# Two unrolled layers, a prologue fed by token blocks, and 512-column up and down matmuls in the last layer

## What is computed

```python
h = concatenate([meta, x], axis=1)                      # 528 tokens
for l in range(2):
    xn = rms_norm(h, attn_norm_g[l])
    q, k, v, u = split(xn @ w_in[l])
    q, k = rope(rms_norm(q)) * q_scale, rope(rms_norm(k))
    h = h + concatenate([sliding_sink_attention(q, k, v, sinks[l]), multiscale_pool(u)]) @ w_out[l]
    xn = rms_norm(h, ffn_norm_g[l])
    g = causal_dwconv(xn @ w_gate[l], conv_w[l], conv_b[l])    # width 3, over tokens
    h = h + (gelu(g) * (xn @ w_up[l])) @ w_down[l]
return h[:, 16:]                                        # the meta tokens are dropped
```

## Time and profile before

| | us |
|---|---|
| three runs | 1168.80, 1163.15, 1167.52 |
| median | 1167.52 |
| span of the profiled execution (its own time was not taken apart from it) | 1165.8 |
| TensorE busy in it | 1125.1 (97%) |
| VectorE, ScalarE, GpSimd busy | 540.5, 472.4, 172.8 |

### The profile page before, as it was taken

The page is one execution under the profiler, slowest core; times in us unless marked ns, Lnnn a source line. Parts: engine busy times, 40 slices in busy tenths (PEclk is TensorE's granted clock), DMA queues, the critical chain, the costliest instruction groups (busy, mean ns, idle before and its releaser), DMA issues.

```text
span 1165.8 us, 21588 instructions
## 1 busy us (share of the span) xinstructions
PE 1125.1 (97%) x8850; PEld 1082.5 (93%) x8850; DVE 540.5 (46%) x663; ACT 472.4 (41%) x652; POOL 172.8 (15%) x138
## 2 busy tenths in 40 slices
PE   4899899999999999999969999999999999999997
PEld 3897699999999999999969876999999999999997
DVE  4666646445454545212157565455544554432222
ACT  3675524544444443111238643353434343421110
POOL 2362003000100010000043510121100110000000
PEclk9989989999999999999989897999999999999999
DMA  5211032322232232233221112223232323233211
GB/s 197 89 46 37 1 109 73 109 73 92 88 108 72 80 100 90 73 100 97 75 74 47 37 37 69 76 74 109 73 107 72 108 72 108 72 100 93 70 63 72
DMA packets 92828, 94.47 MB, mean 81 GB/s; under 512 B 3712, under 2 KB 91096, under 8 KB 92776
## 3 DMA queue, kind: packets, MB, share of 16 engines
q1 hardware_dynamic: 91728, 93.01, 25.0%
q10 hardware_dynamic: 1048, 0.76, 0.2%
HBM read 91.65 MB, written 2.10 MB: 80 GB/s over the span
## 4 chain that ended last, share of the span: by engine, by line
PE 92%; DVE 4%; ACT 2%; issue 2%; DMA 1%; SPq 0%; DVEq 0%; ACTq 0%
PE slot L429 83%; PE slot L573 2%; PE slot L576 2%; DVE x_lo L1009 2%; PE slot L544 1%; PE slot L555 1%; PE slot L481 1%; PE slot L464 1%; DMA x_in<-in_x 1%; DVE ms_work L1075 1%; PE slot L558 1%; DVE sink_all L999 0%; PE slot L667 0%; DVE v_T L1047 0%; ACT rot_s L815 0%
## 5 line engine op out<-in xcount | busy, mean ns | idle before, releaser
L429 PE MATMUL slot<-x_hi,w_hi 128*128 128x264 f32 x1728 | 368.7, 290 | 18.0 <-DVE x_lo L1009 17.9
L429 PE MATMUL slot<-x_lo,w_hi 128*128 128x264 f32 x1728 | 364.0, 288 | 0.0
L429 PE MATMUL slot<-x_hi,w_lo 128*128 128x264 f32 x1728 | 363.9, 288 | 0.0
L343 DVE TENSOR_TENSOR w_lo<-raw,w_hi 128x2048 fp32r<-128x2048 f32 (+2 forms) x86 | 192.8, 2242 | 252.6 <-ACT w_hi L334 252.6
L429 PEld LDWEIGHTS slot<-x_hi,w_hi 128*128 128x128 f32 x1728 | 276.5, 191 | 23.1 <-DVE x_lo L1009 20.7
L334 ACT ACTIVATE w_hi<-raw 128x2048 fp32r<-128x2048 f32 (+3 forms) x90 | 162.6, 1806 | 304.6 <-PE slot L429 297.0
L429 PEld LDWEIGHTS slot<-x_lo,w_hi 128*128 128x128 f32 x1728 | 275.3, 191 | 0.0
L429 PEld LDWEIGHTS slot<-x_hi,w_lo 128*128 128x128 f32 x1728 | 275.0, 191 | 0.0
L429 PE MATMUL slot<-m_hi,w_hi 128*128 128x264 f32 x704 | 143.0, 284 | 0.0
L429 PE MATMUL slot<-m_lo,w_hi 128*128 128x264 f32 x704 | 142.9, 284 | 0.0
L429 PE MATMUL slot<-m_hi,w_lo 128*128 128x264 f32 x704 | 142.6, 284 | 0.0
(11 more groups left out here) (137 smaller groups left out, 1085.8 us busy)
## 6 DMA issues: line engine op xcount, KB each, us to landing
raw<-in_w_gate SPq DMA_DIRECT2D x44, 512.0 KB, 4.4
raw<-in_w_up SPq DMA_DIRECT2D x44, 512.0 KB, 4.6
raw<-in_w_down SPq DMA_DIRECT2D x32, 512.0 KB, 4.0
raw<-in_w_in SPq DMA_DIRECT2D x20, 512.0 KB, 4.8
raw<-in_w_out SPq DMA_DIRECT2D x16, 512.0 KB, 4.0
raw<-in_w_down SPq DMA_DIRECT2D x16, 384.0 KB, 3.5
x_in<-in_x SPq DMA_DIRECT2D x4, 512.0 KB, 5.7
out<-y_out SPq DMA_DIRECT2D x8, 256.0 KB, 2.9
```

Source lines behind the costliest of these rows:

```text
L343: ins = nc.vector.tensor_tensor(w_lo[s][:, a:b], raw[s][:, a:b], w_hi[s][:, a:b].bitcast(f32), ALU.subtract)
L429: ins = nc.tensor.matmul(out_half, w[ws][:, r, cols], a[:, k, half * HALF:(half + 1) * HALF], start=first and n == 0 and w is w_hi and a i ...
```

## The change

Five things are done together.

1. The loop over the layers is written out on all engines (`for l in range(DEPTH)`); waits on counts have constants, and copies of the layer's parameters (`par`, `nsink`, `gain_next`, `gains_all`) go. The MLP and down loops stay.
2. In the last layer, up and down are made for the 512 real tokens: `dense(..., real=True)` writes 512 columns of one bank with one matmul. What works on up, conv, gelu, m and the down sums there takes 512 columns too (`t0 = N_META`). Gate keeps 528.
3. At the end of layer 0, after each pair of down tiles, ScalarE and VectorE make x_hi, x_lo, squares and sums of these two tiles for layer 1, and go on to the next layer's weight units 0 and 1 (`split_hi` and `split_lo` take a unit number past `UNITS`).
4. The sums of squares of both norms are made by VectorE (`add_square`), and GpSimd's low part of the first unit too.
5. The prologue goes by token blocks: eight transposes of block t fill slot t, ScalarE copies half to h and VectorE the other. The k half of the first weight unit is loaded before the third block and split ahead of the v half. q and k norm gains, the sinks and the large table are loaded from GpSimd's queue.

```diff
-    PROLOGUE = [2, 3, 2, 2, 1]
+    PROLOGUE = [1, 1, 1, 2, 1]
...
         def split_hi(act, l, unit, i=0, half=None):
+            if unit >= UNITS:
+                l, unit = l + 1, unit - UNITS
...
         @block.sync
+            kv_cols = blocks(w_in[0])[:, :, ATTN_WIDTH:ATTN_WIDTH + UC]
             for t in range(SEQ // P):
+                if t == 2:
+                    sp.dma_start(raw[0][:, :, 0:P], kv_cols[:, :, 0:P]).then_inc(kraw_loaded, 16)
                 sp.dma_start(x_in[:, t], x[0, t * P:(t + 1) * P, :]).then_inc(x_loaded[t], 16)
+            for a in (0, 4):
+                sp.dma_start(raw[0][:, a:a + 4, P:UC], kv_cols[:, a:a + 4, P:UC]).then_inc(raw_loaded[0], 16)
...
-            sp.wait_ge(par_loaded, 16 * 11)
-            with sp.Fori(0, DEPTH) as l:
+            for l in range(DEPTH):
...
+                if real:
+                    dst = [(slice(N_META, L), slot[s][:, 0, 0:SEQ])]
+                elif part is None:
...
             for k in range(KT):
-                s, feat = (2 + k) % 4, slice(k * P, (k + 1) * P)
...
+            for t in (0, 1, None, 2, 3):
+                if t is None:
+                    pe.wait_ge(par_loaded, 16 * 7)
+                    pe.wait_ge(qk_loaded, 16 * 4)
...
+                pe.wait_ge(x_loaded[t], 16)
+                if t == 3:
+                    pe.wait_ge(evac[3], 1)
+                for k in range(KT):
+                    ins = nc.tensor.transpose(slot[t][:, k // 4, (k % 4) * P:(k % 4 + 1) * P],
+                                              x_in[:, t, k * P:(k + 1) * P], ident)
+                ins.then_inc(filled[t], 1)
+            pe.wait_ge(h_copied, SEQ // P)
...
-            with pe.Fori(0, DEPTH) as l:
+            for l in range(DEPTH):
...
+                        dense(s, unit % 2, (n % 2) * P, eight, x_hi, x_lo, ready=ready if n == 0 else None,
+                              real=n >= 2 and l + 1 == DEPTH).then_inc(filled[s], 1)
...
-                                            m_hi, m_lo, first=n == 0, last=n == 2)
+                                            m_hi, m_lo, first=n == 0, last=n == 2, real=l + 1 == DEPTH)
...
         @block.gpsimd
-            def sum_squares(norm):
...
+            for src, r in ((q_norm_g, R_QG), (k_norm_g, R_KG)):
+                for half in range(2):
+                    pool.dma_start(par_in[r:r + 1, :, half * HEAD_DIM:(half + 1) * HEAD_DIM],
+                                   src.rearrange("(a l) d -> a l d", a=1)).then_inc(qk_loaded, 16)
...
+            pool.dma_start(cst[:, C_CNT:], const[:, C_CNT:]).then_inc(const_loaded, 16)
...
         @block.scalar
+            for t in range(SEQ // P):
+                if t == 2:
+                    act.wait_ge(kraw_loaded, 16)
+                    nc.scalar.activation(w_hi[0][:, :, 0:P], raw[0][:, :, 0:P], ACT.Copy).then_inc(khi_split, 1)
+                act.wait_ge(filled[t], ps.PROLOGUE[t])
...
+            for k in range(KT):
+                gain_hi(0, R_AG, k)
+            act.wait_ge(raw_loaded[0], 32)
+            nc.scalar.activation(w_hi[0][:, :, P:UC], raw[0][:, :, P:UC], ACT.Copy).then_inc(hi_split[0], 1)
+            split_hi(act, 0, 1)
+            for k in range(KT):
+                square(0, 0, k)
+            act.wait_ge(eps_ready, 1)
+            act.wait_ge(prep_ready, 1)
+            act.wait_ge(const_loaded, 16)
...
-                for unit in range(U_DOWN + 2, UNITS):
-                    split_hi(act, l, unit)
+                for j in range(4):
+                    for n in range(3):
+                        if n == 2 and l + 1 < DEPTH:
+                            for k in (2 * j, 2 * j + 1):
+                                act.wait_ge(evac[ps.slot(f"down{k}")], ps.before(f"down{k}", l) + 1)
+                                gain_hi(l + 1, R_AG, k)
+                                square(l + 1, 0, k)
+                        if U_DOWN + 3 * j + n + 2 < UNITS or l + 1 < DEPTH:
+                            split_hi(act, l, U_DOWN + 3 * j + n + 2)
...
         @block.vector
+            def add_square(l, norm, k):
...
+                        if n == 2 and l + 1 < DEPTH:
+                            for k in (2 * j, 2 * j + 1):
+                                gain_lo(l + 1, R_AG, k)
+                                add_square(l + 1, 0, k)
```

245 lines of the change are left out of this document (122 added, 123 removed).

## The result

| | before | after |
|---|---|---|
| runs, taken side by side on one chip | 4 | 4 |
| median, us | 1167.35 | 1126.32 |
| lowest to highest, us | 1163.15 to 1168.80 | 1124.39 to 1129.72 |
| ratio to the kernel before, 95% interval | | 0.9652 (0.9621 to 0.9682) |
| profiled execution: its time, its span | (not apart), 1165.8 | 1127.35, 1125.4 |

The account below looks back on a forecast made before the run. TensorE's own matmul stream was taken to bound the kernel; savings of 30.0 + 12.0 + 11.3 = 53.3 us cut the span from 1165.8 to 1112.5, and 1.7 more gave 1114.2 us, range 1107 to 1130.

Parts of the forecast that it names:

- 512 columns: Last layer's up and down: at 1056 places one 215.8 ns matmul replaces two costing 244.2 ns, saving 30.0 us.
- the column mean: Plain float32 row, 528 column times per weight load, 222.5 ns for 220.0 of columns; gave the 2.5 ns added to 213.3.
- My mechanism: In TensorE's stream, a weight load lasts as long as 264 columns and they interfere; a longer matmul should hide its load.
- Rival 1: In the 512-column matmuls, the 12.1 ns are fixed per matmul, 1124.3 us (15%), or a price per column, 1136.4 us (6%).
- The seam: Between the two layers, 23.75 us for 96 matmuls that need 11.7: no wait left, clock never falls, 12.0 us saved.
- the cover that was counted: At the seam, matmuls of the first six rows, 4.4 us, cover VectorE's 3.3 us for the last two tiles.
- The prologue: Up to the first normalisation: the root begins at 34.6 in place of 45.92, saving 11.3 us.
- Rival 3: The prologue's loads come late; if the root begins at 42 rather than 34.6, the time is 1122 us; 10%.
- Rival 2: Tiles don't come as single matmuls, or the seam stays because x_lo is late on VectorE: 12 less, 1126; 3%.
- rival 4: Second layer's code, fetched anew, stalls TensorE: over 12 stalls lose everything, twenty give 1202 us; 2%.
- The attention: Stretches from each layer's first root or k and v to its gate: forecast saving 0.

Follow-up runs that it names:

- the control: The changed kernel once more, letter for letter, measured beside its successors on one chip: 1130.91 us, ratio 0.9673 to the kernel before.
- the fastest version: Changed kernel with last-layer gate for tokens 12 to 527, sums ahead of unit 1, parameters' wait behind the root, k's weights behind the third block: 1124.17 us.

## Why the prediction was right, and where it was wrong

**512 columns, 30.0 forecast, 13.6 measured: the step that failed.** The count (1056 places) and the price of what was removed (244.2 ns) were right, the price of what was added was not: 231.3 ns in place of 215.8. I took the column mean as the nearest row "in columns per load". It is plain float32, and its column times go at 0.42 ns; a float32r column takes 0.44. The nearest row has to be nearest in number format first. The trace of before offered one float32r length at the high clock, 264, from which fixed and per-column share cannot be told apart; the bounds were 225.4 and 236.8, and that their middle, 231.1, is near the measured price is luck. My mechanism, that at 264 columns the weight load and the columns get in each other's way and that a longer matmul hides its load, fails with it: about 116 of the 122.1 ns are columns, and what comes on top of 0.417 ns a column grows from 12.1 ns at 264 columns to 18.0 at 512 (231.3 - 213.3), where a load that is hidden would have made it shrink. A floor by the load was seen at 128 columns (111.8 ns) and not at 256 (117.6). Rival 1 (15% and 6%) was the right rival, with its two forms mixed. The time lay in the range because the range reached past this rival; the point rested on the wrong price.

**The seam, 12.0 forecast, 12.3 measured.** The x_lo of the last two tiles ran from 575.65 to 577.7 beside the cover that was counted, the clock stayed at 1.00, and the first k matmul followed the last down matmul in the stream. The forecast of the whole was sound because it was made from a measured piece against its steady-state price. The prediction named its causes (idle time, half clock, x_lo slowed by GpSimd) without dividing the 12.0 among them; the rows give 4.2, 4.65 and 3.2 as above.

**The prologue, 11.3 forecast, 11.3 measured,** with small errors that cancelled or lay off the path. VectorE in the changed kernel, what was worked out step by step:

```profile
15.31 0.69 DVE L1011 COPY h<-slot 128x512 f32<-128x512 f32 x1 [1.02 <-PE slot L475]
...
17.05 5.51 DVE L1020 SCALAR_TENSOR_TENSOR x_lo<-h,par_all,x_hi 128x528 fp32r<-128x528 f32 x8
...
24.01 2.29 DVE L345 TENSOR_TENSOR w_lo<-raw,w_hi 128x2048 fp32r<-128x2048 f32 x1 [0.31 <-ACT w_hi L334]
...
27.63 4.77 DVE L1033 TENSOR_TENSOR sumsq<-sumsq,sq 128x528 f32<-128x528 f32 x6 [0.71 <-ACT sq L778]
32.33 0.16 DVE L1046 TENSOR_SCALAR sink_all<-sink_in 128x8 f32<-128x8 f32 x1
```

h was whole at 16.0 (forecast 15.3), k began at 17.95 (17.3), the half clock lasted until 23.35 and not for 16 matmuls, so k and v ended near 32.2 (30.6); but the sums, as counted, ended at 32.4 (32.1) and set the root at 34.63 (34.6). The x_lo began 0.55 us late and took 0.69 in place of 0.76, which made up for it. The blocks did not come later as such: the fourth waited behind the third, and both behind the parameters, whose load from ScalarE's queue is the chain's first long piece:

```profile
3.66 7.53 DMA par_in<-in_conv_w
```

One reading of the old prologue was wrong. VectorE did not hang in L999 (4.36 us) because its tile is 8 elements wide: the same operation took 0.16 us in the changed kernel, above. In the kernel before it lay beside GpSimd's low part of the first unit, and both ended at 25.6:

```profile
21.05 4.52 POOL L688 TENSOR_TENSOR w_lo<-raw,w_hi 128x2048 fp32r<-128x2048 f32 x1 [20.60 <-ACT w_hi L334]
```

So moving that low part to VectorE belongs to the gain of the prologue; no run took this step back alone.

**Rival 3, late loads, came close.** GpSimd's issues (two of the parameters' loads, the first and the third of the sinks, the table):

```profile
2.50 1.00 POOL L690 DMA_DIRECT2D par_in<-in_k_norm_g  x2
10.09 0.65 POOL L694 DMA_DIRECT2D sink_in<-in_sinks  x1 [6.59 <-issue]
19.16 0.60 POOL L694 DMA_DIRECT2D sink_in<-in_sinks  x1 [2.56 <-issue]
25.39 0.59 POOL L697 DMA_DIRECT2D cst<-const_table  x1 [2.55 <-issue]
```

The table takes 6.5 us from issue to landing, so it was there at 31.9, half a microsecond before VectorE was done, and did not set the root. In the run with the sums on GpSimd it did, and in the one with the seam behind down as well (25.03 + 6.77 in its chain, the root at 33.88). The cause of the issue time ahead of each load is open. The Trainium skill ("SBUF — State Buffer", SBUF: two separate sides) describes such loads starved while VectorE copies float32 in a two-port mode. These rows speak against that as the whole cause: the longest gap, 6.59 us, lies before 10.09, and VectorE ran nothing from 1.16 to 11.89; the gaps of 2.5 us lie beside x_lo and w_lo, which are no copies.

**Rival 2 and rival 4** are out: the seam is closed, TensorE's waits after 590 us hold no issue gap except the 0.83 at the tail, and the instruction queue moved 0.46 MB, less than before (0.56). **The attention,** counted at nothing, gave 3.0 us; the rows put it down to the granted clock (0.92 before, 0.94 after), and the control shows that one and the same program differs there by more. That was luck.

## What to carry to other kernels

Price a matmul by rows of its own number format: in float32r a column took 0.44 ns and a matmul 5 to 6 ns on top, in a quiet stretch and in the kernel alike, with 111.8 ns for 128 columns as the least that was seen, so that going from two matmuls to one pays less than not computing the columns. Where a stretch of the chain can be set against its steady-state price (23.75 us for 96 matmuls that need 11.7), the difference is a good forecast for closing it, whatever its causes. And an order belongs to all engines together: edits that moved one engine's step without its partners' (sums behind GpSimd's loads, the root ahead of a split, parameters ahead of a copy) moved a wait to the partner. Where a stretch has many short waits, compare its granted clock before its time.

## What was not expected of the hardware

- A column of float32r costs 0.44 ns at the high clock (121.7, 175.4 and 231.3 ns for 264, 384 and 512), one of bfloat16 0.42 (112.4, 216.0), a column time of plain float32 0.42 (429.2 for 1024), with all else quiet. 128 columns of float32r take 111.8 ns.
- In the prologue the clock starts low: pairs stood 0.44 us apart from 17.95 to 23.35 in the changed kernel, 264 columns at 1.2 GHz. (The stage rows read 1.00 there; they have no change of the clock on record before that rise, so the level is read from the spacing.) In the fastest version pairs stood 0.24 apart from soon after the start (14.93). What the engine did before differs: there it made 16 transposes from 5.20 without a gap, the parameters' right behind, and the next eight at 9.32 in 1.24 us; in the changed kernel every eight took 1.8 to 2.0 us, with gaps of 1.21 and 0.89 us between them. No run varied this alone.
- A stretch of the attention with the same 1108 matmuls took 150.8 to 155.9 us over the runs, at granted clocks from 0.97 down to 0.92, while the MLP behind it took 392.46 us in both executions of the changed kernel.
- VectorE's x_lo took 0.69 us with GpSimd quiet and 1.5 to 1.8 beside its sums, which slowed too (1.3 to 2.0), and an operation of 8 columns took 4.4 us beside one of GpSimd's and 0.16 without.
